# Convolution taps spread over steps 17 to 21, and two rounded weight pieces moved behind the transposed gated rows

## The reference, cut to what matters

```python
proj = u @ w_in                      # 256 x 1024 by 1024 x 3088
c_b, c_c, c_h, q, k, v, g, g_low = split(proj)
y_conv = c_b * causal_depthwise_conv(c_c * c_h, conv_w)   # width 3: taps 0, 1, 2 rows back
o = gated_linear_attention(q, k, v, gates(g_low))
o = o * rsqrt(mean(o * o) + eps) * gla_norm_w * silu(g)   # per head
mix = concat(y_conv, o) @ w_out      # 256 x 1024 by 1024 x 1024
x = layernorm(ALPHA * x + (1 + g1) * mix)
u = x * (1 + sc2) + sh2              # into the feed-forward part
```

## Time and profile before

| | |
|---|---|
| median of 3 runs | 2479.08 us (2474.95 to 2479.88) |
| profiled execution, its own time | 2479.15 us |
| its span | 2477.4 us |
| PE busy | 2384.6 us (96%) |
| DVE busy | 1738.4 us (70%) |
| ACT busy | 1300.5 us (52%) |
| mean granted clock of TensorE | 0.989 |
| first layer's mixer, end of its product with `w_in` | about 142 us |
| second layer's mixer, the same place | about 476 us |

### The profile page before, as it was taken

The page is one execution under the profiler, slowest core; times in us unless marked ns, Lnnn a source line. Parts: engine busy times, 40 slices in busy tenths (PEclk is TensorE's granted clock), DMA queues, the critical chain, the costliest instruction groups (busy, mean ns, idle before and its releaser), DMA issues.

```text
span 2477.4 us, 31241 instructions
## 1 busy us (share of the span) xinstructions
PE 2384.6 (96%) x11448; PEld 1922.4 (78%) x11448; DVE 1738.4 (70%) x1974; ACT 1300.5 (52%) x1661; POOL 81.0 (3%) x135
## 2 busy tenths in 40 slices
PE   7999989999999999999998999999999999999997
PEld 4668866768888888888886888878877887897885
DVE  2588775789999999999986546675467443556556
ACT  2334424458877877777873433554344433444442
POOL 1001000000000000000000000000000000000000
PEclk9999999999999999999999999999999999999998
DMA  9869857659999989989986563355536552337550
GB/s 366 319 233 331 307 210 250 205 175 391 393 325 361 393 310 369 389 310 388 364 299 215 172 211 124 115 195 196 198 134 221 176 209 90 126 112 241 203 187 34
DMA packets 317589, 609.91 MB, mean 246 GB/s; under 512 B 15296, under 2 KB 154592, under 8 KB 310809
## 3 DMA queue, kind: packets, MB, share of 16 engines
q1 hardware_dynamic: 307638, 566.09, 64.5%
q0 software_dynamic: 9552, 41.13, 4.6%
q10 hardware_dynamic: 274, 1.05, 0.1%
HBM read 605.05 MB, written 1.08 MB: 245 GB/s over the span
## 4 chain that ended last, share of the span: by engine, by line
PE 85%; DVE 7%; ACT 3%; DMA 2%; issue 1%; POOL 0%; DVEq 0%; ACTq 0%; SPq 0%
PE G L980 50%; PE A L980 29%; PE TB L980 4%; DMA down<-in_ada_w 1%; PE TB L1468 1%; DVE w_lo L2952 1%; PE TB L1577 1%; DMA down<-in_moe_w_down 1%; PE TB L1002 1%; DVE small L3396 1%; ACT probs L2181 0%; DVE x_tok L3406 0%; DVE l_lo L2913 0%; DVE small L2884 0%; DVE x_tok L3410 0%
## 5 line engine op out<-in xcount | busy, mean ns | idle before, releaser
L980 PE MATMUL G<-w_hi,u_hi 128*128 128x512 f32 x1592 | 621.7, 397 | 4.7 <-ACT u_hi L2523 2.4
L980 PE MATMUL G<-w_hi,u_lo 128*128 128x512 f32 x1592 | 612.1, 391 | 2.9 <-DVE u_lo L3296 2.9
L980 PE MATMUL G<-w_lo,u_hi 128*128 128x512 f32 x1592 | 612.1, 390 | 0.0
L2993 DVE TENSOR_TENSOR w_lo<-wide,w_hi 128x1024 fp32r<-128x1024 f32 x352 | 415.6, 1221 | 13.5 <-ACT w_hi L2249 3.3
L2249 ACT ACTIVATE w_hi<-wide 128x1024 fp32r<-128x1024 f32 x352 | 371.2, 1062 | 89.8 <-PE G L980 43.7
L980 PEld LDWEIGHTS G<-w_hi,u_lo 128*128 128x128 f32 x1592 | 298.7, 188 | 69.3 <-DVE u_lo L3296 5.0
L980 PEld LDWEIGHTS G<-w_hi,u_hi 128*128 128x128 f32 x1592 | 298.6, 188 | 68.9 <-issue 4.1
L980 PEld LDWEIGHTS G<-w_lo,u_hi 128*128 128x128 f32 x1592 | 299.7, 188 | 59.9
L980 PE MATMUL A<-w_hi,hidden_hi 128*128 128x512 f32 x772 | 301.4, 390 | 0.0
L980 PE MATMUL A<-w_hi,hidden_lo 128*128 128x512 f32 x772 | 300.7, 389 | 0.0
L980 PE MATMUL A<-w_lo,hidden_hi 128*128 128x512 f32 x772 | 300.5, 389 | 0.0
(11 more groups left out here) (449 smaller groups left out, 3143.3 us busy)
## 6 DMA issues: line engine op xcount, KB each, us to landing
down<-in_moe_w_down SPq DMA_DIRECT2D x176, 512.0 KB, 8.3
wide<-in_ffn_w_in SPq DMA_DIRECT2D x88, 1024.0 KB, 7.6
wide<-in_moe_w_gate SPq DMA_DIRECT2D x160, 512.0 KB, 8.1
wide<-in_moe_w_up SPq DMA_DIRECT2D x160, 512.0 KB, 9.0
down<-in_ffn_w_out SPq DMA_DIRECT2D x44, 1024.0 KB, 8.5
down<-in_ada_w SPq DMA_DIRECT2D x28, 1024.0 KB, 7.1
wide<-in_w_in SPq DMA_DIRECT2D x24, 1024.0 KB, 7.3
ada_row<-in_ada_w POOLq DMA_DIRECT2D x16, 1024.0 KB, 6.6
```

The costliest lines, as they stand in the source:

```text
L980: return nc.tensor.matmul(o, lhsT, rhs, start=start, stop=stop, skip_group_check=True)
L2993: V.tensor_tensor(w_lo[at % RING][:, :], raw_piece(n, at)[0], w_hi[at % RING][:, :].bitcast(F32), ALU.subtract).then_inc(lo_ready, 1)
```

## The change

Three things are moved; nothing is computed otherwise.

1. VectorE: `conv_term(0)` from step 18 to 17, `conv_term(1)` from 20 to 18 (behind `mean_square(0)`), `conv_term(2)` from 20 to 19 (behind `normed(0)`), `conv_add(1)` from 21 to 20 (behind `normed(1)`). `conv_add(2)` stays at 21.
2. VectorE at p = 24: the two `lower_half` of the gated rows come between `out_rest(1)` and `out_rest(2)`.
3. ScalarE: pieces 2 and 3 of `w_out` are rounded behind the two copies of the transposed gated rows, ahead of piece 4.

```diff
@@ ScalarE, behind the copies of the transposed rows @@
                         if before == "gla" and i == 1:
+                            layer = plan[index - 1][1]
+                            act.wait_ge(gla_conv_read, T * (layer + 1))
+                            act.wait_ge(gla_y, T * (layer + 1))
+                            mixer_out_piece(m, 2)
+                            mixer_out_piece(m, 3)
                             mixer_out_piece(m, 4)
                             mixer_out_piece(m, 5)
@@ ScalarE, end of the mixer's steps @@
                     mixer_out_piece(out, 0)
                     mixer_out_piece(out, 1)
-                    act.wait_ge(gla_conv_read, T * (arg + 1))
-                    act.wait_ge(gla_y, T * (arg + 1))
-                    mixer_out_piece(out, 2)
-                    mixer_out_piece(out, 3)
@@ VectorE, between(c, q) @@
-                        if p == 18:
+                        if p == 17:
                             dve.wait_ge(s_gla, 32 * (arg + 1))
                             conv_term(0)
+                        if p == 18:
                             mean_square(0)
+                            conv_term(1)
                         if p == 19:
                             mean_square(1)
                             normed(0)
+                            conv_term(2)
                         if p == 20:
                             normed(1)
-                            conv_term(1)
-                            conv_term(2)
+                            conv_add(1)
                         if p == 21:
-                            conv_add(1)
                             conv_add(2)
...
                         if p == 24:
-                            for at in range(4):
+                            for at in (0, 1):
                                 out_rest(at)
                             for i in range(T):
                                 lower_half("trs8", steps[index + 1][2], i, 2, "gla")
+                            for at in (2, 3):
+                                out_rest(at)
```

## The result

The changed kernel takes 2482.48 us (median of 13 runs, 2480.67 to 2488.12); the kernel before, measured beside it, takes 2476.79 us (13 runs, 2474.95 to 2479.88). The ratio is 1.0021 with a 95% interval of 1.0014 to 1.0028, so the kernel is slower by about 0.2%, 5.7 us by the medians. The profiled execution has a span of 2481.8 us where it was 2477.4, 4.4 us more.

A forecast was written before the change was run, and what follows sets the result against it. TensorE, busy 96%, was taken to bound the kernel, with waits in the second mixer and the first layer's modulation rows. Second mixer -2.5, read +6.3, clock +1.0 gave +4.8, so 2483.9 us; range 2476.5 to 2488.

The forecast's parts named there:

- The failed step: First mixer, step 19: shifts land at 120.5, so rest of piece 19 ends 0.3 us late, bounds 0 and 0.8.
- The second failed step: First layer, modulation rows: late reads share the engines with SP's loads, delaying `fold` by 6.3 us, between 2.6 and 8.3.
- the landing of the write: First layer: 8 KB write held until SP's later burst is through, landing at about 151.0 instead of 148.4.
- a read that lands within 6 us of its issue: First layer, sign against the forecast: the kernel then doesn't change measurably or gets a little faster.
- rival C: First layer: read leaves late but is served first, +2.6, no clock loss; no change, 2479.2 us; chance 0.20.
- The clock: First layer, behind TensorE's roughly 7 us idle: lower granted clock costs +1.0 us, bounds 0 and 3.
- Second mixer: Product with `w_out` starts 2.5 us earlier despite a new wait before step 19: -2.5 us, bounds -3.4 and -1.4.
- The order of rests 2 and 3: First layer: rests 2 and 3 behind the low halves make GpSimd's write leave at 144.8, 1.6 us late.
- B: First layer: read held until SP's 3 MB are through, +10, clock +2; 2488.5 us; chance 0.15.
- D: First layer: write not held, landing at 146.7; faster, 2475.3 to 2480.0, middle 2477.6 us; chance 0.15.
- A: The forecast itself: the read shares the engines with SP's loads; 2481 to 2487 us; chance 0.45.

The follow-up runs named there:

- Run 2: Kernel before with only the low halves ahead of rests 2 and 3 and ScalarE's reordered rounding, taps and sums as before: 2478.96 us, ratio 0.9999.
- Run 5: Run 2 with the first layer's sum of the modulation rows put ahead of the fourth rest: 2474.79 us, ratio 0.9988.
- Run 3: The changed kernel with the six shifting copies put ahead of the first 1 MB of `w_out` in SP's queue: 2479.61 us, ratio 1.0001.
- run 4: The changed kernel with tap 1 waiting only for its own three copies, tap 2 for the others on a second semaphore: 2478.74 us, ratio 1.0002.
- run 1: Kernel before with only the taps and sums moved, rests and low halves in the old order: 2486.76 us, ratio 1.0030.
- run 6: Run 5 with tap 0 at step 17, taps 1 and 2 at steps 19 and 20, sums at 21 and 23: 2475.33 us, ratio 0.9989.

## Why the prediction came out right in size and wrong in its way

**The failed step.** "With landing at 120.5 the rest of piece 19 ends 0.3 us after TensorE wants it. Bounds 0 and 0.8." This is a term of the sum that was mis-sized: the copies landed at 123.4, TensorE stood 3.1 us, and the clock cost 1.6 more; the gated rows came 4.8 us late, for 0.3. I had read the 80% busy queue at 120 to 121 us as the end of the copies and let the bounds depend on it, though I wrote that the rows don't say whose packets these are. Only in the second mixer did a window show the queues empty; there tap 1 was forecast for 457.15 and came at 457.7 after the shift of 6.8 us. For the first mixer I had no landing of a copy at all. The trace of before did have the landing of the 1 MB load that stands right in front of them: issued at 109.30, it took 10.1 us, until 119.4. A landing of the six copies behind it 1.1 us later was thus a guess without a row.

**The second failed step.** The reads beside SP's loads: "The case at hand is nearer to the second row; I take two thirds of the way". That put 3.7 us into the sum beyond the late start of the reads (two thirds of the way from 2.6 to 8.3 are 6.4, not 6.3, a slip without weight). Run 2 shows 0: `fold` follows the reads by 6.02 us. The premise behind it failed first. I let the landing of the write move with the start of SP's burst, 2.7 us late; in run 2 it moved 1.3 with the write's own issue, and the write's packets went before SP's last ones. So the reads kept 1.16 us of lead over the next load. In the change itself SP's loads moved as well, since they hang on rest 7, which hung on the late TensorE: lead 0.84 us, no slowing. Run 5 gives the price that the lead hides, 2.5 us at a lead of 0.04.

**Errors that met.** The first layer was forecast at +6.3 and measured at +6.55, out of other terms: 4.8 + 1.25 + 0.4 for the write and 0.1 for the reads, against 0.3 + 1.3 + 1.05 + 3.65. That the median lies 1.4 us from the forecast (and its distance to before 0.9 us from the 4.8 of the sum) says nothing for the working: it is luck. One of the signs that the forecast gave for being wrong did come, a read that lands within 6 us of its issue (5.5 us in the change, from 155.65), and the late copies alone kept the kernel from the result named there, no measurable change. Run 3, where the copies are early, is the case that I had described: it loses 1.95 us in the first layer, and its time cannot be told from before's. That is rival C, and without the late copies C would have been the result.

**The clock.** +1.0 us behind the transposes was wrong, 0 measured: the clock did fall, but the wait of 1.75 us hid all of it. The loss by the clock came elsewhere, at step 19, behind 3.1 us of idle time that the forecast didn't have.

**Second mixer.** Mechanism right, size a little off: -2.5 forecast, with bounds of -3.4 and -1.4, and -1.83 measured. The new wait before step 19 is there, 1.22 us for 1.0; the wait before the product with `w_out` is gone. The two short waits of 0.36 and 0.28 us lie in the forecast's times as well, which start steps 20 and 21 3.3 us apart, as measured. What is off is their place: copies that landed 0.6 us later than taken shift all that follows. With the copies' landing out of the way, by the semaphores of run 4, the gain is 3.24, near the forecast's bound for early shifts. The halves alone gain 1.93 there (run 2), the taps alone lose 2.17 (run 1), since the wait of 2.02 us before the product stays and the clock falls behind it. Together they give -1.83: beside the halves, late taps add nothing; with the copies first they add 0.7 (run 3, -2.62).

**What was right.** The order of rests 2 and 3 delays the write by 1.25 us (1.3 forecast beside the 0.3). The write waits for SP's loads in front of it; run 5 shows it by taking them away, 2.02 us for 5.5. That it waits for the end of the burst was wrong (run 2). No run here tests the statement of the Trainium skill that the forecast weighed there ("DMA: Bandwidth & Descriptors", Queues, rings and completion order: the increment lands behind every earlier write of the DMA engine, across its queues), since the write's packets were late themselves. By the other statement of that section, that the engines take their queues in turn packet by packet, the write's packets would have gone in run 2 about as soon as in run 5, where they move 1.0 to 1.5 us after its issue. The trace doesn't agree: they moved 4.0 to 4.7 us after it.

**Rivals.** B (reads held until SP's 3 MB are through) and D (write not held) are refuted by the change's own rows. A held by its total only.

## What to carry to other kernels

Moving a consumer of a DMA earlier is priced by when that DMA lands, so find the landing of that very transfer (or of its like behind the same load) before counting the slack; where the trace has only waits that were never reached, take the longest landing behind a load of that size as the bound. Look at what stands in front in the queue first: moving six copies ahead of one 1 MB load, or an 8 KB write ahead of a 2 MB burst, was worth 4.6 us and 2.2 us in the first layer here. And a stall of TensorE of 2 to 3 us may have to be counted with its clock (1.6 us behind 3.1 us of idle time here), unless another wait follows that would swallow it.

## What was not expected of the hardware

- Copies from SBUF to SBUF were counted as landed 8.6 us after the last issue behind a 1 MB load, and 5.1 us without it; three of the six, by their own semaphore, 2.0 us ahead of all six.
- An 8 KB write took 5.5 us behind 2 MB of another queue's loads, though its packets moved 1 us and more before the last of theirs (run 2), and 2.0 us when they were issued 2 us after it (run 5).
- Behind 3.10 us of TensorE's idle time the granted clock was 0.54 (the change) and behind 2.02 us 0.55 (run 1, where three shorter waits came before); behind 1.08 us it stayed at 1.00 (run 4). Yet behind 2.29 us before the transposes of the first layer it stayed at 1.00 as well (run 3, the eight matmuls took 2.08 us), and behind 2.55 us there it fell (the change). The length of a stall alone doesn't tell whether the clock falls.
- The clock did not fall alike in each profile for the same steps. At the start of the second mixer before's window shows 0.57 where that of the halves alone shows 1.00 (windows of before, then of run 2):

```profile
392.00:396.00 4.00, 4.00 (x13) 3.20 (x13) 0.65 (x1) 1.74 (x4) 0.00 (x0) 0.57 0.65 246
```

```profile
392.00:396.00 4.00, 3.76 (x21) 3.32 (x22) 1.41 (x2) 2.77 (x5) 0.00 (x0) 1.00 0.85 261
```

Run 2 started its last modulation product 0.5 us earlier than before, though its first layer was 1.3 us behind, which fits this clock. So single profiles differ by about 2 us far from any edit, which is why the table takes the two places one by one. Five of the ten profiles have such a fall between 392 and 404 us: before, the change and runs 3, 4 and 6. The other five have none, and from the power of the first layer to the last modulation product they are 1.8 to 2.2 us quicker than before, where the five with a fall are between 0.6 quicker and 0.2 slower. It thus comes with the change and without it; what sets it off, and how often it comes in the runs that weren't profiled, stays open.
